# TensorE sums the squares of three norms between the last products of the layer before

## The chip, the cores and the metric

The kernel runs on one core of one Trainium2 chip. The time is the device time of one execution in microseconds (us). The engines are TensorE (PE, with its weight loads PEld), VectorE (DVE), ScalarE (ACT), GpSimd (POOL) and SyncE (SP), which issues most DMAs. Each engine works through its own instructions in order; semaphores tie them together.

## The reference

The reference is a two-layer diffusion backbone over 256 context and 256 latent tokens with 1024 features. Layer 0 has windowed attention beside a gated DeltaNet, layer 1 a Mamba-2 mixer, and each layer ends in a convolutional FFN. What matters here is the RMSNorm ahead of each projection and the residual that feeds it:

```python
def rms_norm(x, g):
    xf = x.astype(f32)
    y = xf * lax.rsqrt(jnp.mean(xf * xf, axis=-1, keepdims=True) + EPS)
    return (y * g.astype(f32)).astype(x.dtype)
...
        x = x + gt1 * m_lat
        x = x + gt2 * conv_ffn(modulate(rms_norm(x, norm_ffn_g[i]), sh2, sc2),
                               ffn_up[i], ffn_conv[i], ffn_down[i])
...
    return rms_norm(x, final_g)
```

The mean of the squares runs over all 1024 features of a token.

## The kernel before

The residual stream lies in SBUF as `xT`, features on the partitions, in eight blocks of 128 features by 512 tokens (256 context, 256 latent). A product that ends in the residual is a `RowGemm`. It reads the weights slot by slot. A slot holds two blocks of 128 input features, split into a high and a low part: ScalarE writes `w_hi`, VectorE writes `w_lo` (`split_lo`, line 304). TensorE makes three matmuls for each pair (high by high, L568; high by low activations, L571; low by high, L572). Except in the last slot it goes through the eight output blocks for each input block. In the last slot the output block m is outermost: six matmuls finish it and raise `mm_done`, then the next block follows. Each output block has one of the eight PSUM banks, in the order of `ROW_BANKS`: bank 4 for m = 0.

Behind each finished block comes a small pipeline. VectorE evicts the block into `xT` (L958; one instruction for each 256 tokens), ScalarE squares it into `norm_sq`, a ring of two buffers (L975), and VectorE adds the first six squared blocks into `norm_acc`, five additions in all (L982), each of them queued between two evictions. Ahead of the first eviction VectorE has one more weight split in its queue: that of the first slot of the next stage.

When all products are out, `Norm.pe_sums` has TensorE sum over the partitions with a matrix of ones: once for `norm_acc` (blocks 0 to 5), once for block 6 and once for block 7 (L1011). The output of each of the groups of 128 tokens goes to its own 32 partitions of bank 4, so a matmul there takes 32 columns of the array. An fp32 matmul stands as two records in the trace. ScalarE takes the root (L1018), VectorE the reciprocal (L1024), TensorE spreads the result over 128 partitions (`pe_spread`, L1030). Then VectorE and ScalarE make the modulated activations block by block (`norm_xn` L1044, `h_hi` L1063, `h_lo` L1052), TensorE multiplies the first weight slot with each block as it comes (`pe_first_slot`), and behind the last block VectorE splits the second weight slot, for which TensorE's next products wait.

Three norms are of this kind, each after a `RowGemm`: the first after the output projection of layer 0 (512 tokens, around 702 to 717 us of the profile), the second after the FFN of layer 0 (512 tokens, around 1075 to 1090), and the third after the output projection of layer 1 (256 tokens, around 1546 to 1555). The last norm (`Final`) uses the same class `Squares` but does its own sums. It is written as before in both kernels.

The order of each engine's work is written out by hand in `stage_layer0_tail` and `stage_layer1_tail`; there is no planner.

Of the kernel before, what the change touches and what calls it, by code (L numbers as in the profile page):

```python
# [19 lines left out]
P = 128  # L20
D = 1024
KD = D // P
# [101 lines left out]
class Tally:  # L124


    def __init__(self, sem):
        self.sem, self.base = sem, 0
# [7 lines left out]
    def take(self, n):  # L136

        self.base += n
        return Mark(self.sem, self.base - n)
# [116 lines left out]
def issue_loads(k, sp, upto):  # L256

    s = k.stream
    upto = min(upto, len(s.plan))
    while s.issued < upto:  # L260
        g = s.issued
        kind, n, parts = s.plan[g]
        if g >= 2:
            was, m, _ = s.plan[g - 2]
            if was == "split":
                sp.wait_ge(k.hi_done.sem, m + 1)
                sp.wait_ge(k.lo_done.sem, m + 1)
            else:
                sp.wait_ge(k.mod_used.sem, m + 1)
        for part in parts:  # L270
            if part[0] in ("rows", "rows4"):
                dst = s.raw[:, g % 2, :].rearrange("p (k n) -> p k n", k=4 if part[0] == "rows4" else 2)
                if part[1] is not None:
                    dst = dst[part[1] * HD:part[1] * HD + HD]
                src = part[2]
            else:
                (c0, w), src = part
                dst = s.raw[:, g % 2, :].rearrange("p (k n) -> p k n", k=KD)[:, :, c0:c0 + w]
            sp.dma_start(dst, src).then_inc(s.landed[g % 2], 16)
        s.issued += 1  # L280
# [683 lines left out]
class Squares:  # L964


    def __init__(self, k, row, sq, acc, sq_done, acc_done):
        self.k, self.row, self.sq, self.acc, self.sq_done, self.acc_done = k, row, sq, acc, sq_done, acc_done

    def act_square(self, act, m):  # L970
        k = self.k
        act.wait_ge(self.row.out_done.sem, self.row.out_done.at(m + 1))
        if m >= 2:
            act.wait_ge(self.acc_done.sem, self.acc_done.at(max(1, m - 2)))
        act.activation(self.sq[:, m % 2, :], k.xT[:, m, self.row.t0:T], ACT.Square).then_inc(self.sq_done.sem, 1)  # L975

    def dve_add(self, dve, j):
# [6 lines left out]
    def dve_evict_and_add(self, dve):  # L984
        for m in range(KD):
            self.row.dve_evict(dve, m)
            if 2 <= m <= 6:
                self.dve_add(dve, m - 1)


class Norm:
# [3 lines left out]
    def __init__(self, k, layer, which, row, hT, lT, b):  # L995
        self.k, self.layer, self.which, self.row = k, layer, which, row
        self.t0, self.n = row.t0, row.n
        self.hT, self.lT, self.xn, self.r = hT, lT, b.xn, b.r
        self.nt = self.n // P
        (sq_done, acc_done, self.sum_done, self.root_done, self.recip_done, self.spread_done, self.xn_done, self.hi_done,  # L1000
         self.lo_done) = take(k.tallies["norm"] + k.tallies["xnorm"], (KD, 5, 1, 1, 1, 1, KD, KD, KD))
        self.squares = Squares(k, row, b.sq, b.acc1, sq_done, acc_done)
        self.sum_bank, self.rstd_bank = k.pb[4], k.pb[5]

    def pe_sums(self, pe):
        k, q = self.k, self.squares
        parts = [(q.acc_done, 5, q.acc[:, :]), (q.sq_done, 7, q.sq[:, 0, :]), (q.sq_done, 8, q.sq[:, 1, :])]
        for i, (done, n, src) in enumerate(parts):
            pe.wait_ge(done.sem, done.at(n))
            for t in range(self.nt):  # L1010
                mm = pe.matmul(self.sum_bank[32 * t:32 * t + 32, 0:P], k.ones[:, 0:32], src[:, t * P:t * P + P],  # L1011
                               start=(i == 0), stop=(i == 2))
        mm.then_inc(self.sum_done.sem, 1)

    def act_root(self, act):
        k, rows = self.k, 32 * self.nt
        act.wait_ge(self.sum_done.sem, self.sum_done.at(1))
        act.activation(self.r[0:rows, :], self.sum_bank[0:rows, 0:P], ACT.Sqrt, bias=k.eps[0:rows, 0:1],  # L1018
                       scale=1.0 / D).then_inc(self.root_done.sem, 1)

# [301 lines left out]
class Final:  # L1322
# [18 lines left out]
    def pe_after(self, pe, m):  # L1341
        if m >= 5:
            self.pe_turn(pe, m - 5)
# [942 lines left out]
def stage_layer0_tail(k, a, g_out, g_up, g_down, g_ssm, cat, h, gh, gl, b):  # L2286


    nc = k.nc
    with ExitStack() as st:  # L2290
        row0 = RowGemm(k, 0, 2, g_out, 4, cat, 0, opens=True)
        norm1 = Norm(k, 0, 1, row0, h[0], h[1], b)
        up = FfnUp(k, 0, g_up, norm1, gh, gl, b.acc)
        down = RowGemm(k, 0, 5, g_down, KF // 2, lambda c: (gh(c), gl(c)), 0, up=up)
        norm2 = Norm(k, 1, 0, down, h[0], h[1], b)
        ssm = SsmIn(k, a, g_ssm, norm2, b)
        block = st.enter_context(nc.Block())

        @block.sync
        def _(sp):  # L2300
            issue_loads(k, sp, g_ssm + ssm.n_slots + 2)

        @block.tensor
        def _(pe):
            row0.pe(pe)
            norm1.pe(pe)
            up.pe(pe)
            down.pe(pe)
            norm2.pe(pe)
            ssm.pe(pe)  # L2310

        @block.scalar
        def _(act):
            row0.act_splits(act, 1, 5)
            norm1.act(act)
            up.act(act)
            down.act_splits(act, 1, KF // 2 + 1)
            norm2.act(act)
            ssm.act(act)

        @block.vector
        def _(dve):
            row0.dve_splits(dve, 1, 5)
            norm1.dve(dve)
            up.dve(dve)
            down.dve_splits(dve, 1, KF // 2 + 1)
            norm2.dve(dve)
            ssm.dve(dve)

    ssm.gates.end()  # L2330


def stage_layer1_tail(k, g_sout, g_up, g_down, y, h, gh, gl, b, out):

    nc = k.nc
    with ExitStack() as st:
        row1 = RowGemm(k, 1, 2, g_sout, SI // P // 2, y, LC, opens=True)
        norm = Norm(k, 1, 1, row1, h[0], h[1], b)
        up = FfnUp(k, 1, g_up, norm, gh, gl, b.acc)
        down = RowGemm(k, 1, 5, g_down, KF // 2, lambda c: (gh(c), gl(c)), LC, up=up)  # L2340
        fin = Final(k, down, b.sq, b.acc1, b.xs, b.xg, b.ss)
        block = st.enter_context(nc.Block())

        @block.sync
        def _(sp):
            issue_loads(k, sp, len(k.stream.plan))
            for h_ in range(2):
                sp.wait_ge(fin.y_done.sem, fin.y_done.at(h_ + 1))
                sp.dma_start(out[0, 0:P, h_ * 512:h_ * 512 + 512], fin.xg[:, 0, h_ * 512:h_ * 512 + 512]).then_inc(fin.s_out.sem, 16)
                sp.wait_ge(fin.y1_done.sem, fin.y1_done.at(h_ + 1))  # L2350
                sp.dma_start(out[0, P:2 * P, h_ * 512:h_ * 512 + 512], fin.xg[:, 1, h_ * 512:h_ * 512 + 512]).then_inc(fin.s_out.sem, 16)
            sp.wait_ge(fin.s_out.sem, fin.s_out.at(64))

        @block.tensor
        def _(pe):
            row1.pe(pe)
            norm.pe(pe)
            up.pe(pe)
            down.pe(pe, after=fin.pe_after)
            fin.pe_tail(pe)  # L2360

        @block.scalar
        def _(act):
            row1.act_splits(act, 1, SI // P // 2 + 1)
            norm.act(act)
            up.act(act)
            down.act_splits(act, 1, KF // 2)
            fin.act(act)

        @block.vector  # L2370
        def _(dve):
            row1.dve_splits(dve, 1, SI // P // 2 + 1)
            norm.dve(dve)
            up.dve(dve)
            down.dve_splits(dve, 1, KF // 2)
            fin.dve(dve)
# [196 lines left out]
```

## Time and profile before

| what | value |
|---|---|
| time, median of 3 runs | 1755.87 us (1751.68 to 1760.56) |
| profiled execution, time | 1765.24 us |
| its span, first to last instruction | 1763.2 us |
| mean granted TensorE clock, as a share of 2.4 GHz | 0.899 |
| TensorE busy (matmul) | 1525.8 us, 87% |
| VectorE busy | 989.7 us, 56% |
| ScalarE busy | 589.0 us, 33% |

The busy shares are those of the whole span. A norm takes some 15 us of it, so what limits a norm has to be read in its own stretch. The granted clock is either 1.00 or 0.50 at a given moment; a stretch with a change in it shows a value between.

### The profile page before, as it was taken

The page shows a single profiled execution, that of the slowest core. Times are in us where ns is not written, and L with a number is a line of the kernel's source. Part 1 is how long each engine was busy: PE and PEld are TensorE (multiplying, and loading weights), DVE is VectorE, ACT ScalarE, POOL GpSimd, SP SyncE. Part 2 cuts the span into 40 slices and gives each one's busy share as a digit, 9 for nine tenths or more (in the row PEclk, how much of TensorE's full clock was granted, in tenths as well). Part 3 has the DMA queues.
Part 4 walks back from the last instruction along what each step waited for, and adds up shares of the span by engine and source line. Part 5 has one row for each costly group of instructions (what it writes and reads, how often), then busy time and mean ns, then how long its engine had stood idle before and what let it go on. Part 6 is the DMA issues. An engine that isn't in the chain of part 4 may idle for free. (4 is left out here: it accounts for less than half of the span.)

```text
span 1763.2 us, 29502 instructions
## 1 busy us (share of the span) xinstructions
PE 1525.8 (87%) x12916; PEld 1252.5 (71%) x12916; DVE 989.7 (56%) x1457; ACT 589.0 (33%) x863; POOL 42.5 (2%) x42
## 2 busy tenths in 40 slices
PE   4499995779999759799999998999777975989998
PEld 2376772567777637688888886888755764979998
DVE  3346531464553452766555226767769666378854
ACT  2423435212222032533333113445211114355544
POOL 0000000000000000000000000000001210000000
PEclk8699997679999989899999998999897666989999
DMA  5622110025566203233332321322410000546653
GB/s 201 154 79 72 29 48 31 1 98 193 193 208 226 50 2 103 64 96 96 96 98 93 110 100 54 108 96 87 135 48 1 1 1 1 172 134 177 188 167 120
DMA packets 170618, 173.24 MB, mean 98 GB/s; under 512 B 15254, under 2 KB 135802, under 8 KB 170362
## 3 DMA queue, kind: packets, MB, share of 16 engines
q1 hardware_dynamic: 169184, 170.38, 31.0%
q8 instruction: 102, 1.67, 0.4%
q10 hardware_dynamic: 1306, 0.97, 0.2%
q14 instruction: 26, 0.21, 0.0%
HBM read 170.29 MB, written 1.05 MB: 97 GB/s over the span
## 5 line engine op out<-in xcount | busy, mean ns | idle before, releaser
L304 DVE TENSOR_TENSOR w_lo<-w_raw,w_hi 128x2048 fp32r<-128x2048 f32 x99 | 225.2, 2275 | 207.3 <-ACT w_hi L294 207.3
L568 PE MATMUL bank<-h_hi,w_hi 128*128 128x512 f32 (+1 forms) x904 | 316.1, 350 | 9.9 <-DVE h_lo L1052 7.5
L572 PE MATMUL bank<-h_hi,w_lo 128*128 128x512 f32 (+1 forms) x904 | 313.7, 347 | 0.0
L571 PE MATMUL bank<-h_lo,w_hi 128*128 128x512 f32 (+1 forms) x904 | 313.6, 347 | 0.0
L294 ACT ACTIVATE w_hi<-w_raw 128x2048 fp32r<-128x2048 f32 x99 | 187.9, 1898 | 225.0 <-PE bank L568 219.9
L586 DVE SCALAR_TENSOR_TENSOR acc<-bank,params,acc 128x510 f32<-128x510 f32 (+3 forms) x272 | 173.7, 646 | 131.1 <-ACT acc L1158 95.7
L568 PEld LDWEIGHTS bank<-h_hi,w_hi 128*128 128x128 f32 x904 | 173.1, 191 | 32.1 <-issue 11.7
L572 PEld LDWEIGHTS bank<-h_hi,w_lo 128*128 128x128 f32 x904 | 172.8, 191 | 21.2
L571 PEld LDWEIGHTS bank<-h_lo,w_hi 128*128 128x128 f32 x904 | 173.0, 191 | 20.5
L1158 ACT ACTIVATE acc<-bank,params 128x512 f32<-128x512 f32 (+1 forms) x88 | 49.3, 582 | 192.6 <-PE bank L572 90.8
L568 PE MATMUL bank<-h_hi,w_hi_hyb 128*128 128x512 f32 (+1 forms) x184 | 78.3, 426 | 21.9 <-PEq L476 19.8
L1653 PEld LDWEIGHTS bank<-inv_T,X_mat 64*64 64x64 f32 x1280 | 70.1, 136 | 13.2 <-issue 12.8
L1653 PE MATMUL bank<-inv_T,X_mat 64*64 64x64 f32 x1280 | 76.6, 225 | 1.2 <-issue 1.1
L571 PE MATMUL bank<-h_lo,w_hi_hyb 128*128 128x512 f32 (+1 forms) x184 | 74.5, 405 | 0.0
L572 PE MATMUL bank<-h_hi,w_lo_hyb 128*128 128x512 f32 (+1 forms) x184 | 74.3, 404 | 0.0
L1655 PE MATMUL bank<-X_mat,inv_T 64*64 64x64 f32 x1024 | 66.9, 223 | 2.0 <-issue 2.0
L1655 PEld LDWEIGHTS bank<-X_mat,inv_T 64*64 64x64 f32 x1024 | 62.7, 140 | 2.8 <-issue 2.8
L431 PE MATMUL bank<-w_raw,cond_padded 128*32 128x512 f32 x384 | 54.0, 673 | 9.4 <-DMA w_raw<-in_mod_w 7.2
L2124 PEld LDWEIGHTS bank<-x_dt,ssd_decay 128*128 128x128 f32 x256 | 41.0, 248 | 27.3 <-issue 21.6
L568 PEld LDWEIGHTS bank<-h_hi,w_hi_hyb 128*128 128x128 f32 (+1 forms) x184 | 35.6, 194 | 33.7 <-issue 23.1
L2124 PE MATMUL bank<-x_dt,ssd_decay 128*128 128x64 f32 x256 | 42.0, 334 | 19.9 <-DVE ssd_decay L2197 10.3
L304 DVE TENSOR_TENSOR w_lo_hyb<-w_raw,w_hi_hyb 128x2048 fp32r<-128x2048 f32 (+1 forms) x12 | 25.8, 2149 | 59.1 <-ACT w_hi_hyb L294 59.1
(349 smaller groups left out, 2881.9 us busy)
## 6 DMA issues: line engine op xcount, KB each, us to landing
w_raw<-in_mod_w SPq DMA_DIRECT2D x48, 1024.0 KB, 6.1
w_raw<-in_ffn_up SPq DMA_DIRECT2D x88, 512.0 KB, 5.1
w_raw<-in_ffn_down SPq DMA_DIRECT2D x22, 1024.0 KB, 4.9
w_raw<-in_ssm_w_in SPq DMA_DIRECT2D x20, 1024.0 KB, 5.2
w_raw<-in_hyb_w_in SPq DMA_DIRECT2D x9, 1024.0 KB, 5.1
w_raw<-in_ssm_w_out SPq DMA_DIRECT2D x8, 1024.0 KB, 4.9
w_raw<-in_hyb_w_in SPq DMA_DIRECT2D x8, 256.0 KB, 5.0
w_raw<-in_hyb_w_out SPq DMA_DIRECT2D x4, 512.0 KB, 7.9
```

Of the source, the lines that this page charges most:

```text
L294: act.activation(hi, raw, ACT.Copy).then_inc(k.hi_done.sem, 1)
L304: dve.tensor_tensor(lo, raw, hi.bitcast(F32), ALU.subtract).then_inc(k.lo_done.sem, 1)
L431: mm = pe.matmul(k.pb[7][32 * j:32 * j + 32, :], k.condpad[:, 4 * half + j, :], w[:, j, :], start=(half == 0), stop=(half == 1))
L568: mm = pe.matmul(out, wh, xh, start=(start and n == 0), stop=False)
L571: pe.matmul(out, wh, xl, start=False, stop=False)
L572: mm = pe.matmul(out, wl, xh, start=False, stop=(stop and n == last))
L586: ins = dve.scalar_tensor_tensor(out=ao, in0=bo, scalar=w(j), in1=ao, op0=ALU.mult, op1=ALU.add)
L1158: act.activation(acc[:, i % 4, :], self.bank(i), ACT.Copy, scale=self.taps(i)(1)).then_inc(self.seed_done.sem, 1)
L1653: mm = pe.matmul(YT(l)[q, r * DNC:r * DNC + DNC], Xm[q, l, r, :], d.TT[q, n, r, :], start=True, stop=True)
L1655: mm = pe.matmul(Y(l)[q, r * DNC:r * DNC + DNC], d.TT[q, n, r, :], Xm[q, l, r, :], start=True, stop=True)
L2124: mm = pe.matmul(k.pb[4 + q % 2][:, o:o + 64], dec[:, j % 2, dr, h, :], xdt[:, dr, (8 * g) * 64 + o:(8 * g) * 64 + o + 64], start=(dr == 0 ...
```

## The change

In the three norms TensorE now sums each of the eight squared blocks by itself: eight groups of matmuls of the ones matrix in place of three. The sums of blocks 0 to 5 stand in TensorE's queue inside the last slot of the products: behind the products of output block m comes the sum of squared block m - 2. Blocks 6 and 7 are summed after the last products. VectorE's five additions are gone, and `norm_acc` is no longer written by these norms. A buffer of `norm_sq` comes free when TensorE has summed it. The last norm keeps its additions.

```diff
@@ class Squares
-    def __init__(self, k, row, sq, acc, sq_done, acc_done):
+    def __init__(self, k, row, sq, acc, sq_done, acc_done, on_pe=False):
+        self.on_pe = on_pe
...
         act.wait_ge(self.row.out_done.sem, self.row.out_done.at(m + 1))
         if m >= 2:
-            act.wait_ge(self.acc_done.sem, self.acc_done.at(max(1, m - 2)))
+            act.wait_ge(self.acc_done.sem, self.acc_done.at(m - 1 if self.on_pe else max(1, m - 2)))
...
         for m in range(KD):
             self.row.dve_evict(dve, m)
-            if 2 <= m <= 6:
+            if 2 <= m <= 6 and not self.on_pe:
                 self.dve_add(dve, m - 1)
@@ class Norm
+    def pe_sum(self, pe, m):
+        k, q = self.k, self.squares
+        pe.wait_ge(q.sq_done.sem, q.sq_done.at(m + 1))
+        for t in range(self.nt):
+            mm = pe.matmul(self.sum_bank[32 * t:32 * t + 32, 0:P], k.ones[:, 0:32], q.sq[:, m % 2, t * P:t * P + P],
+                           start=(m == 0), stop=(m == KD - 1))
+        mm.then_inc(q.acc_done.sem, 1)
+
+    def pe_after(self, pe, m):
+        if m >= 2:
+            self.pe_sum(pe, m - 2)
+
     def pe_sums(self, pe):
-        k, q = self.k, self.squares
-        parts = [(q.acc_done, 5, q.acc[:, :]), (q.sq_done, 7, q.sq[:, 0, :]), (q.sq_done, 8, q.sq[:, 1, :])]
-        for i, (done, n, src) in enumerate(parts):
-            pe.wait_ge(done.sem, done.at(n))
-            for t in range(self.nt):
-                mm = pe.matmul(self.sum_bank[32 * t:32 * t + 32, 0:P], k.ones[:, 0:32], src[:, t * P:t * P + P],
-                               start=(i == 0), stop=(i == 2))
-        mm.then_inc(self.sum_done.sem, 1)
+        self.pe_sum(pe, 6)
+        self.pe_sum(pe, 7)
 
     def act_root(self, act):
...
-        act.wait_ge(self.sum_done.sem, self.sum_done.at(1))
+        act.wait_ge(self.squares.acc_done.sem, self.squares.acc_done.at(KD))
@@ stage_layer0_tail
-            row0.pe(pe)
+            row0.pe(pe, after=norm1.pe_after)
...
-            down.pe(pe)
+            down.pe(pe, after=norm2.pe_after)
@@ stage_layer1_tail
-            row1.pe(pe)
+            row1.pe(pe, after=norm.pe_after)
```

`RowGemm.pe` calls `after(pe, m)` behind the products of each output block of the last slot.

## Rows read from the trace of the kernel before

**Rows 1.** The page, part 1: busy time and share of each engine.

```profile
...
PE 1525.8 (87%) x12916; PEld 1252.5 (71%) x12916; DVE 989.7 (56%) x1457; ACT 589.0 (33%) x863; POOL 42.5 (2%) x42
...
```

**Rows 2.** Chain of work that ended last, behind the third norm: start, us, what.

```profile
...
1563.79 2.30 DVE w_lo L304
1566.23 0.36 PE bank L568
...
```

**Rows 3.** Timeline, first norm: start, us, engine, line, work [idle before <- releaser].

```profile
...
701.66 0.39 PE L572 MATMUL bank<-cat_dn_hi,w_lo 128*128 128x512 f32 x1
...
702.52 2.44 DVE L958 SCALAR_TENSOR_TENSOR xT<-bank,mod,xT 128x256 f32<-128x256 f32 x6
...
703.43 1.42 ACT L975 ACTIVATE norm_sq<-xT 128x512 f32<-128x512 f32 x2 [1.70 <-DVE xT L958]
...
708.46 0.39 PE L572 MATMUL bank<-cat_dn_hi,w_lo 128*128 128x512 f32 x1
...
711.09 0.87 DVE L958 SCALAR_TENSOR_TENSOR xT<-bank,mod,xT 128x256 f32<-128x256 f32 x2
...
711.23 0.43 PE L1011 MATMUL bank<-norm_acc,ones 128*32 128x128 f32 x8 [2.38 <-DVE norm_acc L982]
...
711.48 0.40 PE L1011 MATMUL bank<-norm_sq,ones 128*32 128x128 f32 x8
...
712.68 0.65 PE L1011 MATMUL bank<-norm_sq,ones 128*32 128x128 f32 x8 [0.80 <-ACT norm_sq L975]
...
714.81 2.08 PE L1030 MATMUL bank<-norm_r,base_consts 128*128 128x128 f32 x8 [1.48 <-DVE norm_r L1024]
...
```

**Rows 4.** Timeline, second norm, first squares.

```profile
...
1074.84 0.39 PE L572 MATMUL bank<-ffn_g_hi_b,w_lo 128*128 128x512 f32 x1
...
1076.60 0.63 ACT L975 ACTIVATE norm_sq<-xT 128x512 f32<-128x512 f32 x1 [1.70 <-DVE xT L958]
...
```

**Rows 5.** Timeline, second norm, VectorE's last eviction.

```profile
...
1084.26 0.48 DVE L958 SCALAR_TENSOR_TENSOR xT<-bank,mod,xT 128x256 f32<-128x256 f32 x1
...
```

**Rows 6.** Timeline of TensorE, third norm, end of the third product.

```profile
...
1543.73 0.28 PE L572 MATMUL bank<-y_hi,w_lo 128*128 128x256 f32 x1
...
```

**Rows 7.** Timeline of ScalarE, third norm, first squares.

```profile
...
1546.82 0.81 ACT L975 ACTIVATE norm_sq<-xT 128x256 f32<-128x256 f32 x2 [2.74 <-DVE xT L958]
...
```

**Rows 8.** Timeline, third norm, last eviction and spread.

```profile
...
1551.15 0.48 DVE L958 SCALAR_TENSOR_TENSOR xT<-bank,mod,xT 128x256 f32<-128x256 f32 x1
...
1554.21 1.22 PE L1030 MATMUL bank<-norm_r,base_consts 64*128 64x128 f32 x4 [1.44 <-DVE norm_r L1024]
...
```

**Rows 9.** Timeline of TensorE, modulation stage, between two tilings.

```profile
...
565.49 1.07 PE L431 MATMUL bank<-w_raw,cond_padded 128*32 128x512 f32 x8 [0.59 <-DMA w_raw<-in_mod_w]
566.49 0.34 PE L1653 MATMUL bank<-inv_T,X_mat 64*64 64x64 f32 x4
...
```

**Rows 10.** Timeline of TensorE, last FFN's products.

```profile
...
1692.77 0.28 PE L571 MATMUL bank<-ffn_g_lo,w_hi 128*128 128x256 f32 x1
1692.89 0.28 PE L572 MATMUL bank<-ffn_g_hi,w_lo 128*128 128x256 f32 x1
1695.14 0.36 PE L568 MATMUL bank<-ffn_g_hi,w_hi 128*128 128x256 f32 x1 [1.97 <-issue]
...
```

**Rows 11.** Busy time by stretch (the x is a count), PEclk is the granted clock.

```profile
...
core 0: us, PE busy (x) PEld busy (x) DVE busy (x) ACT busy (x) POOL busy (x), PEclk, DMA share, GB/s
...
1688.00:1695.40 7.40, 5.43 (x46) 5.26 (x45) 4.89 (x8) 2.94 (x4) 0.00 (x0) 1.00 0.34 135
1695.50:1698.80 3.30, 3.30 (x17) 3.30 (x17) 1.20 (x1) 1.91 (x1) 0.00 (x0) 0.50 0.80 238
1698.90:1705.00 6.10, 6.10 (x53) 6.10 (x53) 1.15 (x2) 1.92 (x1) 0.00 (x0) 1.00 0.62 208
...
```

**Rows 12.** The same view, two stretches after the first norm's products.

```profile
...
708.85:712.40 3.55, 0.65 (x17) 0.38 (x16) 3.11 (x7) 1.66 (x3) 0.00 (x0) 1.00 0.00 0
712.45:719.20 6.75, 2.73 (x16) 1.98 (x16) 3.04 (x7) 1.92 (x6) 0.00 (x0) 0.50 0.00 0
...
```

More of the change, by code:

```diff
@@ L1000, in __init__ @@
         (sq_done, acc_done, self.sum_done, self.root_done, self.recip_done, self.spread_done, self.xn_done, self.hi_done,
-         self.lo_done) = take(k.tallies["norm"] + k.tallies["xnorm"], (KD, 5, 1, 1, 1, 1, KD, KD, KD))
-        self.squares = Squares(k, row, b.sq, b.acc1, sq_done, acc_done)
+         self.lo_done) = take(k.tallies["norm"] + k.tallies["xnorm"], (KD, KD, 0, 1, 1, 1, KD, KD, KD))
+        self.squares = Squares(k, row, b.sq, b.acc1, sq_done, acc_done, on_pe=True)
         self.sum_bank, self.rstd_bank = k.pb[4], k.pb[5]
-    def pe_sums(self, pe):
-        k, q = self.k, self.squares
-        parts = [(q.acc_done, 5, q.acc[:, :]), (q.sq_done, 7, q.sq[:, 0, :]), (q.sq_done, 8, q.sq[:, 1, :])]
-        for i, (done, n, src) in enumerate(parts):
-            pe.wait_ge(done.sem, done.at(n))
-            for t in range(self.nt):
-                mm = pe.matmul(self.sum_bank[32 * t:32 * t + 32, 0:P], k.ones[:, 0:32], src[:, t * P:t * P + P],
-                               start=(i == 0), stop=(i == 2))
-        mm.then_inc(self.sum_done.sem, 1)
+    def pe_sum(self, pe, m):
[8 more added lines that the diff above has]
+            self.pe_sum(pe, m - 2)
+    def pe_sums(self, pe):
+        self.pe_sum(pe, 6)
+        self.pe_sum(pe, 7)
     def act_root(self, act):
         k, rows = self.k, 32 * self.nt
-        act.wait_ge(self.sum_done.sem, self.sum_done.at(1))
+        act.wait_ge(self.squares.acc_done.sem, self.squares.acc_done.at(KD))
         act.activation(self.r[0:rows, :], self.sum_bank[0:rows, 0:P], ACT.Sqrt, bias=k.eps[0:rows, 0:1],
```

## The prediction

> **What bounds the kernel now.** The page's busy shares come first: TensorE is busy for 87% of the span [rows 1], so almost everywhere a delay of TensorE is a delay of the end. The chain of waits comes second. Behind the third norm it runs through VectorE's split of the second weight slot (1563.79, 2.30 us) into TensorE's next products at 1566.23 [rows 2]. That split stands behind the eight modulated blocks in VectorE's queue, and they stand behind the spread of the root. So whatever moves the spread moves the next stage by the same amount, and the first slot's products, which run beside the modulation, do not set its end. The timeline comes third, for what sets the spread. In the first norm TensorE has issued its last product matmul at 708.46 (it ends 0.39 later, at 708.85), while VectorE starts its last eviction only at 711.09 [rows 3]. VectorE is behind: its first eviction starts at 702.52, because a weight split stands ahead of it, and three evictions take 2.44 us, 0.81 each. Seven steps of 0.81 would be 5.7 us; the last eviction starts 8.57 us after the first, and the difference, 2.9 us, is the five additions (0.58 each). From the last eviction the path is eviction, square, sum, root, reciprocal, spread.
>
> So the change takes work off the engine that is late. The question is what it puts on TensorE, and where.
>
> **What TensorE waits for.** The sum of block 0 stands behind the third product block. In the first norm that block's last matmul starts at 701.66 and ends at 702.05. The square of block 0 starts at 703.43 [rows 3] and one of 512 tokens takes 0.63 [rows 4]. From the end of the last eviction (711.96) to the last sum (712.68) pass 0.72 us: a square and two handovers, 0.05 each [rows 3]. So the first sum can start at 703.43 + 0.63 + 0.05 = 704.11, and TensorE, which before worked through, stands 2.06 us with products 3 to 7 queued behind. The removed additions do not help here: the first of them came after three evictions. In the second norm it is the same: block 2 ends at 1074.84 + 0.39 = 1075.23, the sum can start at 1076.60 + 0.63 + 0.05 = 1077.28 [rows 4], a stall of 2.05. In the third (256 tokens) block 2 ends at 1544.01 [rows 6], the square starts at 1546.82 and takes half of 0.81 [rows 7], so the sum starts at 1547.28, a stall of 3.27. Who is late next: product blocks 3 to 7, and with them VectorE's last five evictions.
>
> **What a sum costs between products.** Two groups of sums in a row start 0.25 us apart at the full clock (711.23, 711.48) [rows 3]; four matmuls of 32 columns each run at the same time, so the third norm with two of them pays the same. Turning from 32-column tiles to another tiling costs more: eight records of 512 columns start at 565.49 and the next tiling at 566.49 [rows 9]. By the sums' price those columns are four times 0.22 plus a start of 0.03, 0.91; the turn is the remaining 0.09, rounded to 0.10. I take that for the turn back too. The first product after a break takes 0.36 in place of 0.28 [rows 10]: 0.08 more for a weight load that nothing hides. A sum between products is 0.25 + 0.10 + 0.10 + 0.08 = 0.53 us; the first one, after a stall, has no turn into it: 0.43. From below the turns are free and a sum is 0.25. From above each turn waits out a whole matmul (0.39), and a sum is 1.11. I take 0.53, since the row that shows a turn is nearest to it.
> The Trainium skill, TensorEngine Tiling (Array Packing), Key Properties, says that a change of the tiling mode drains the engine. It speaks against this change: without a drain the sums cost 3.7 us in all below, with it 7.6. The trace agrees with a drain, at 0.09 us for the turn that it shows.
>
> **The sum, norm by norm, at the full clock.** From matmul 18 of the last slot (701.66) to matmul 48 (708.46) are 6.80 us, which is the work of product blocks 3 to 7 [rows 3]. Their last matmul ends 0.39 - 0.23 = 0.16 after its slot in the stream. With four more sums between the five blocks the last product is done at 704.11 + 0.43 + 6.80 + 4 x 0.53 + 0.16 = 713.62, and the last eviction starts 0.05 later, at 713.67, against 711.09: **2.58 us later**. The evictions of 0.87 and squares of 0.63 keep up with a product block every 1.89, so TensorE alone paces it. The sum of block 5 is done before the last square is. Second norm: 1077.28 + 9.51 + 0.05 = 1086.84 against 1084.26 [rows 5]: 2.58. Third: the matmuls start 0.12 apart [rows 10], 30 of them are 3.60; 1547.28 + 0.43 + 3.60 + 2.12 + 0.16 + 0.05 = 1553.64 against 1551.15 [rows 8]: 2.49. Together +7.6 us (7.65).
>
> **The clock.** Two terms more. First, a stall inside the products can bring the granted clock down from 2.4 to 1.2 GHz. In the last FFN TensorE stood from 1693.17 to 1695.14, 1.97 us [rows 10]. The clock was 1.00 before, 0.50 in 1695.5 to 1698.8, and 1.00 after, and TensorE got 17 matmuls done in those 3.3 us where at the rate after (53 in 6.1) it would be 29 [rows 11]: 12 x 0.12 = 1.4 us lost, or half of 3.3, 1.65. I take 1.6 for each fall. The stalls here are 2.05, 2.06 and 3.27 us. I take the longest and one of the other two: +3.2. Bounds: none, 0; three, +4.8. Second, today the clock falls at the end of the norm: 1.00 until 712.4 with TensorE 0.65 us busy in 3.55, then 0.50 [rows 12]. The last sum takes 0.65 where at the full clock one takes 0.40 (0.25), and the spread takes 2.08 [rows 3], in the third norm 1.22 [rows 8], half of it at the full clock. After the change TensorE has just finished its products when the last square comes (some 1.5 us later), so the last sum most likely runs at the full clock in all three: -0.75. For the spread it is open, as TensorE idles again during root and reciprocal; I take it as won in one large and in the third norm: -1.04 - 0.61. Together -2.4. Bounds: 0 and -3.4.
>
> **Nothing else moves.** No DMA is added or moved; the weights' release comes with the first matmul of the slot, ahead of the stall, so SyncE's queue is untouched. ScalarE's squares wait for a sum in place of an addition and are not late by it. VectorE's added idle time is worth nothing.
>
> Sum: 7.6 + 3.2 - 2.4 = **+8.4 us** on the profiled execution's 1765.24. It lies 9.4 us above the median of the runs, and most of that has nothing to do with three norms, so I put the 8.4 on the median: 1755.87 + 8.4 = **1764.3 us**.
>
> **Rivals.**
> - *Turns are free* (a sum is 0.25): 0.18 + 4 x 0.28 = 1.30 less per norm, 3.9 in all: +4.5, 1760.4 us. Against it speaks the turn seen, though in another pair of tilings.
> - *The clock holds through the stalls*: 7.6 - 2.4 = +5.2, 1761.1 us. For it: two stalls are barely longer than 2 us. Against it: the fall after 1.97 us.
> - *The clock falls in all three and nothing is won at the end*: 7.6 + 4.8 = +12.4, 1768.3 us. It takes no more than the same row three times.
> - *The first sum never waits* (faster). If the squares were ready when block 2 ends, only five sums of 0.53 would push the products: the last eviction at 708.85 + 2.65 + 0.05 = 711.55 (+0.46), in the second norm 6.80 + 2.70 after 1075.23, 1084.73 (+0.47), in the third the products, before done 30 x 0.12 after 1544.01 at 1547.61, at 1550.31 (-0.84). That is +0.1, and with the whole clock gain -3.3: 1752.6 us. With free turns as well (about -7.4) it would near the faster side of what can be told. It needs the first eviction 2.06 us earlier, in the third norm 3.27; the sign turns at a stall of about 1.1 us per norm (3.3 / 3). The split ahead of the evictions is not moved, so I give it little.
>
> **How the numbers follow.** A measurement of this kernel tells no change from about 0.5%, 8.8 us. Forecast (one or two falls of the clock, +6 to +11) 0.50; free turns 0.16; clock holds 0.12; three falls 0.18; first sum without a wait 0.04. The forecast's interval lies about half above 8.8: slower 0.22 + 0.18 = 0.40, rounded up to 0.42 for turns dearer than 0.10. The last rival alone reaches beyond 8.8 on the faster side only with free turns, so faster is 0.03 at most; same 0.55. The range goes from the free turns with the clock gain taken at its best (3.7 - 3.4, about 0) and a little of the runs' own scatter to the three falls and as much: 1757 to 1770 us. Turns of 0.39, some +15, are left out.
>
> **What would show it.** TensorE's timeline in the last slot: a gap of about 2.05, 2.05 and 3.3 us behind matmul 18, named as a wait for ScalarE's square; five groups of sums at some 0.5 us each between product blocks; the last eviction (L958) waiting for a matmul and no longer for its own queue; the granted clock at 0.50 somewhere behind a gap; spreads nearer 1 than 2 us. From the last split's end to the spread's start some 2.5 us more in each norm. The prediction fails if the gaps are missing, if a sum between products is far from 0.5, or if the delay is swallowed ahead of the second slot's products.

## The result

The changed kernel takes 1765.45 us in the median (1763.98 to 1772.70, 8 runs), the kernel before 1755.09 (1749.29 to 1760.56, 8 runs). The ratio is 1.0065, with a 95% interval of 1.0042 to 1.0088: slower by 11.4 us, between 7.4 and 15.5. The two medians differ by 10.4 us; every such difference in us in this document is the ratio's, taken on the median of the kernel before. The forecast was +8.4 us and 1764.3 us.

The first view is the page of the kernel after: its head and the busy time of the engines.

```profile
span 1764.3 us, 29675 instructions
...
PE 1531.7 (87%) x13016; PEld 1251.2 (71%) x13016; DVE 982.7 (56%) x1442; ACT 588.4 (33%) x863; POOL 42.5 (2%) x42
...
```

The span is only about 1 us longer than that of [rows 1]'s execution, and TensorE's share is the same. The two spans can't be held against each other for this change: before's profiled execution was a long one of its kind (1765.24 us against a median of 1755), and the first norm's last slot begins at 692.23 here and at 697.81 there, ahead of anything that was changed. So each norm is measured by itself, from the first product matmul of the last slot to the first matmul of the second weight slot of the next stage:

| us from first matmul of the last slot to | norm 1 before | norm 1 after | norm 2 before | norm 2 after | norm 3 before | norm 3 after |
|---|---|---|---|---|---|---|
| last eviction | 13.28 | 17.60 | 13.28 | 16.16 | 9.45 | 13.38 |
| spread | 17.00 | 21.09 | 17.00 | 19.65 | 12.52 | 16.21 |
| second slot's first matmul | 35.79 | 39.89 | 35.80 | 38.44 | 24.53 | 28.23 |

The last line adds up to 96.12 us before and 106.56 after. The three norms alone are 10.4 us longer, and that is the measured slowdown within its interval.

Next the second norm in TensorE's timeline of the kernel after. It is the one in which the clock stayed up. L1010 are the sums, L1037 is the spread.

```profile
...
1073.37 0.39 PE L572 MATMUL bank<-ffn_g_hi_b,w_lo 128*128 128x512 f32 x1
1075.81 0.43 PE L1010 MATMUL bank<-norm_sq,ones 128*32 128x128 f32 x8 [2.06 <-ACT norm_sq L976]
...
1077.43 0.39 PE L572 MATMUL bank<-ffn_g_hi_b,w_lo 128*128 128x512 f32 x1
1077.75 0.43 PE L1010 MATMUL bank<-norm_sq,ones 128*32 128x128 f32 x8
...
1085.24 0.39 PE L572 MATMUL bank<-ffn_g_hi_b,w_lo 128*128 128x512 f32 x1
1085.56 0.65 PE L1010 MATMUL bank<-norm_sq,ones 128*32 128x128 f32 x16
1087.26 0.42 PE L1010 MATMUL bank<-norm_sq,ones 128*32 128x128 f32 x8 [1.05 <-ACT norm_sq L976]
1089.16 2.07 PE L1037 MATMUL bank<-norm_r,base_consts 128*128 128x128 f32 x8 [1.48 <-DVE norm_r L1031]
```

Product block 2 ends at 1073.37 + 0.39 = 1073.76, and then TensorE does nothing until 1075.81, when the first square is there (before, products ran through here, [rows 4]). From there a sum stands between product blocks with a period of 1.94 us (1075.81, 1077.75) in place of 1.36. The spread takes 2.07 us, as in [rows 3].

VectorE in the same stretch:

```profile
...
1072.02 2.29 DVE L304 TENSOR_TENSOR w_lo<-w_raw,w_hi 128x2048 fp32r<-128x2048 f32 x1 [8.59 <-ACT w_hi L294]
1074.23 2.44 DVE L958 SCALAR_TENSOR_TENSOR xT<-bank,mod,xT 128x256 f32<-128x256 f32 x6
1077.86 0.88 DVE L958 SCALAR_TENSOR_TENSOR xT<-bank,mod,xT 128x256 f32<-128x256 f32 x2 [1.20 <-PE bank L572]
...
1085.67 0.88 DVE L958 SCALAR_TENSOR_TENSOR xT<-bank,mod,xT 128x256 f32<-128x256 f32 x2 [1.08 <-PE bank L572]
...
```

Ahead of the first eviction stands the weight split (1072.02, 2.29 us). Three evictions run in a row as before, then each waits about 1.1 us for TensorE's matmul (L572). Before, the last one waited for VectorE's own queue [rows 3, 5]. The engine that was late is now idle, and the engine that has the products is late.

The busy time by stretch, with the granted clock (the number behind the ACT count and POOL's), for the first, second and third norm:

```profile
...
696.40:698.50 2.10, 0.07 (x1) 0.00 (x0) 2.10 (x5) 0.63 (x1) 0.00 (x0) 1.00 0.05 14
699.65:703.00 3.35, 3.35 (x15) 1.95 (x14) 0.88 (x2) 1.02 (x2) 0.00 (x0) 0.50 0.77 216
703.05:709.70 6.65, 6.65 (x46) 4.01 (x45) 2.63 (x6) 1.90 (x3) 0.00 (x0) 1.00 0.01 2
...
1073.80:1075.80 2.00, 0.00 (x0) 0.00 (x0) 2.00 (x6) 0.63 (x1) 0.00 (x0) 1.00 0.23 30
1075.85:1085.60 9.75, 9.75 (x74) 6.03 (x76) 4.32 (x11) 3.79 (x6) 0.00 (x0) 1.00 0.31 103
1085.65:1088.70 3.05, 0.98 (x24) 0.44 (x24) 1.42 (x3) 1.00 (x2) 0.00 (x0) 1.00 0.00 0
1088.80:1090.00 1.20, 0.84 (x4) 0.84 (x5) 0.31 (x1) 0.00 (x0) 0.00 (x0) 0.50 0.00 0
...
1542.55:1545.80 3.25, 0.00 (x0) 0.00 (x0) 3.17 (x4) 0.51 (x3) 0.00 (x0) 1.00 0.47 124
1546.15:1549.50 3.35, 3.35 (x17) 2.74 (x16) 0.48 (x1) 0.84 (x3) 0.00 (x0) 0.50 0.99 282
...
```

The gaps are there in all three. In the first norm the clock was 0.50 from 699.65 to 703.00, with TensorE at work (15 matmul records in 3.35 us, eight of them those of a sum); in the second it stayed at 1.00; in the third it was 0.50 from 1546.15 to 1549.50. At the end of the norm it fell again, in the second between 1088.70 and 1088.80, just ahead of the spread. The first norm's spread, at 713.32, was slow as well (TensorE's timeline):

```profile
...
713.32 2.08 PE L1037 MATMUL bank<-norm_r,base_consts 128*128 128x128 f32 x8 [1.47 <-DVE norm_r L1031]
...
```

The sums of the third norm, in TensorE's timeline of the kernel after. From 1546.15 to 1549.50 the clock is 0.50, behind that it is 1.00:

```profile
...
1545.82 0.41 PE L1010 MATMUL bank<-norm_sq,ones 128*32 128x128 f32 x4 [3.27 <-ACT norm_sq L976]
...
1547.74 0.64 PE L1010 MATMUL bank<-norm_sq,ones 128*32 128x128 f32 x4
...
1549.76 0.41 PE L1010 MATMUL bank<-norm_sq,ones 128*32 128x128 f32 x4
...
1550.99 0.41 PE L1010 MATMUL bank<-norm_sq,ones 128*32 128x128 f32 x4
...
1552.24 0.41 PE L1010 MATMUL bank<-norm_sq,ones 128*32 128x128 f32 x4
...
1554.59 0.41 PE L1010 MATMUL bank<-norm_sq,ones 128*32 128x128 f32 x4 [0.46 <-ACT norm_sq L976]
...
```

At the full clock a product block of 256 tokens and its sum take 1.25 us (1550.99, 1552.24), where six product matmuls 0.12 apart are 0.72: a sum costs 0.53 here.

### The profile page after: what moved, and what is told of

Read it like the earlier page. It is cut to its first block and busy times, and to the rows that moved or that the text cites. A ratio compares the mean times of both kernels' runs of the same rounds, so it can differ in the third digit from the quotient of the medians.

```text
span 1764.3 us, 29675 instructions
## 1 busy us (share of the span) xinstructions
PE 1531.7 (87%) x13016; PEld 1251.2 (71%) x13016; DVE 982.7 (56%) x1442; ACT 588.4 (33%) x863; POOL 42.5 (2%) x42
## 3 DMA queue, kind: packets, MB, share of 16 engines
HBM read 170.29 MB, written 1.05 MB: 97 GB/s over the span
## 5 line engine op out<-in xcount | busy, mean ns | idle before, releaser
L572 PE MATMUL bank<-h_hi,w_lo 128*128 128x512 f32 (+1 forms) x904 | 313.6, 347 | 0.0
L572 PEld LDWEIGHTS bank<-h_hi,w_lo 128*128 128x128 f32 x904 | 172.8, 191 | 21.6
L572 PE MATMUL bank<-h_hi,w_lo_hyb 128*128 128x512 f32 (+1 forms) x184 | 73.2, 398 | 0.0
```

Source lines behind the costliest of these rows:

```text
L572: mm = pe.matmul(out, wl, xh, start=False, stop=(stop and n == last))
```

## The experiments

Six more kernels ran, each beside the kernel before on the same chip. The column "norms" is the sum over the three norms of the stretch above, from one profiled execution, less the 96.12 us of the kernel before.

| kernel | ratio to before (95%) | us from it | norms, us |
|---|---|---|---|
| changed kernel | 1.0065 (1.0042 to 1.0088) | +11.4 | +10.4 |
| e1: all sums behind the products | 0.9935 (0.9914 to 0.9956) | -11.4 | -9.5 |
| e2: e1 and the wait alone | 1.0008 (0.9986 to 1.0030) | +1.4 | +0.9 |
| e3: e1 and sums five blocks behind | 0.9967 (0.9946 to 0.9988) | -5.8 | -6.3 |
| e5: changed kernel, weight split behind the evictions | 1.0022 (0.9999 to 1.0046) | +3.9 | +2.9 |
| e6: changed kernel, idle filled at the end | 1.0071 (1.0037 to 1.0106) | +12.5 | +9.6 |
| e4: e1, idle filled at the end | 0.9947 (0.9930 to 0.9964) | -9.3 | -9.4 |

**e1: all sums behind the products.** The squares get eight buffers, so neither ScalarE nor TensorE has to wait for the other until the end:

```diff
-            act.wait_ge(self.acc_done.sem, self.acc_done.at(m - 1 if self.on_pe else max(1, m - 2)))
-        act.activation(self.sq[:, m % 2, :], ...
+            if not self.on_pe:
+                act.wait_ge(self.acc_done.sem, self.acc_done.at(max(1, m - 2)))
+        act.activation(self.sq[:, m % (8 if self.on_pe else 2), :], ...
...
     def pe_after(self, pe, m):
-        if m >= 2:
-            self.pe_sum(pe, m - 2)
+        pass
 
     def pe_sums(self, pe):
-        self.pe_sum(pe, 6)
-        self.pe_sum(pe, 7)
+        for m in range(KD):
+            self.pe_sum(pe, m)
```

> All eight sums of a norm stand behind the last product, none between products; the squares have a buffer each, so that no square waits. Theory (the time went into TensorE's wait inside the products, the turns of tiling between them, and the clock's falls behind the wait): no gap inside the products; the last eviction starts with the last product's end, about 2.15 us earlier than in the kernel before in each norm, and the last sum runs at the full clock (0.25 us less): about -7 us against the kernel before, 1748. Rival (the additions' removal or something outside the norms made it slower, not the place of the sums): about +10 us against the kernel before, as in the changed kernel.

Measured: 1745.63 us in the median, 0.9935. TensorE's timeline of the second norm in e1:

```profile
...
1065.91 0.39 PE L572 MATMUL bank<-ffn_g_hi_b,w_lo 128*128 128x512 f32 x1
1066.23 2.13 PE L1011 MATMUL bank<-norm_sq,ones 128*32 128x128 f32 x64
1069.84 1.16 PE L1037 MATMUL bank<-norm_r,base_consts 128*128 128x128 f32 x8 [1.48 <-DVE norm_r L1031]
```

VectorE's, and the busy time by stretch behind the products:

```profile
...
1066.34 0.88 DVE L958 SCALAR_TENSOR_TENSOR xT<-bank,mod,xT 128x256 f32<-128x256 f32 x2 [0.48 <-PE bank L572]
...
```

```profile
...
1066.30:1069.80 3.50, 2.06 (x65) 1.56 (x64) 1.83 (x3) 1.22 (x3) 0.00 (x0) 1.00 0.02 5
1069.80:1071.00 1.20, 1.16 (x8) 0.97 (x8) 0.00 (x0) 0.00 (x0) 0.00 (x0) 1.00 0.00 0
...
```

The last eviction starts with the end of the last product (1066.34 against 1065.91 + 0.39); in the third norm, where the products are shorter, VectorE is still 1.4 us behind. All eight sums take 2.13 us, 64 records, most of it in time in which TensorE had nothing else. The spread takes 1.16 us with the clock at 1.00, and so in all three norms (1.16, 1.16, 0.71). The rival falls: the additions' removal is worth 2.2 us a norm once nothing takes their place on TensorE. The gain is larger than I expected (-11.4 against -7, the norms -9.5) by the spreads at the full clock (0.92 + 0.92 + 0.51 = 2.4 us), which I had left open.

**e2: the wait alone.** As e1, and behind the third product block TensorE waits for the first square without summing it:

```diff
     def pe_after(self, pe, m):
-        pass
+        if m == 2:
+            pe.wait_ge(self.squares.sq_done.sem, self.squares.sq_done.at(1))
```

> As e1, but TensorE waits for the first square behind the third product block, without any sum there. Theory: gaps of 2.06, 2.06 and 3.27 us stand behind matmul 18 of the last slot; the last eviction starts 2.06 us (3.27 less 1.4 of cover by VectorE's evictions in the third norm) later than in e1, plus up to 1.7 us for each fall of the clock: +6 to +11 us against e1, so about +2 us against the kernel before. Rival (the sums' own time and turns cost it, the wait is covered by VectorE's lateness): the same time as e1 within 1 us.

Measured: 1.0008, +1.4 us, that is +12.8 against e1 by the ratios (11.5 by the medians) and +10.4 by the norms. Busy time by stretch in e2, first, second and third norm:

```profile
...
697.85:699.80 1.95, 0.00 (x0) 0.00 (x0) 1.95 (x5) 0.61 (x1) 0.00 (x0) 1.00 0.07 20
701.05:704.35 3.30, 3.30 (x10) 2.53 (x9) 0.88 (x2) 0.97 (x2) 0.00 (x0) 0.50 0.78 221
...
1071.70:1073.60 1.90, 0.00 (x0) 0.00 (x0) 1.90 (x5) 0.59 (x1) 0.00 (x0) 1.00 0.22 13
1073.70:1080.70 7.00, 7.00 (x30) 5.55 (x30) 4.35 (x11) 3.48 (x6) 0.00 (x0) 1.00 0.43 145
1540.70:1543.90 3.20, 0.00 (x0) 0.00 (x0) 3.14 (x4) 0.46 (x3) 0.00 (x0) 1.00 0.59 164
1544.10:1547.40 3.30, 3.30 (x16) 3.30 (x17) 1.09 (x3) 1.06 (x4) 0.00 (x0) 0.50 0.94 271
...
```

The gaps are back, with no matmul in them, and behind them the clock fell in the first and the third norm, not in the second. The second norm gives the price of the wait at the full clock: 34.81 - 32.45 = 2.36 us for a gap of 2.06. The first gives 36.43 - 32.45 = 3.98, so the fall cost 1.62. The rival, that VectorE's lateness covers the wait, falls. The +1.4 against the kernel before is not told apart from zero: the wait alone eats what taking the additions away gives.

**e3: sums between products, without a wait.** As e1, and the sums of blocks 0 to 2 stand behind product blocks 5 to 7:

```diff
     def pe_after(self, pe, m):
-        pass
+        if m >= 5:
+            self.pe_sum(pe, m - 5)
 
     def pe_sums(self, pe):
-        for m in range(KD):
+        for m in range(3, KD):
             self.pe_sum(pe, m)
```

> As e1, but the sums of blocks 0 to 2 stand behind the products of blocks 5 to 7: turns between products without a wait in the norms of 512 tokens (the third norm keeps some 1.3 us of it). Theory: each sum between products costs 0.58 us (a period of 1.95 us per product block and sum, against 1.36 for the block alone); the last eviction starts 1.2 us later than in e1: about +3 us against e1, -4 against the kernel before. Rival (a sum between products costs only its columns, 0.22 us): +1 us against e1.

Measured: 0.9967, -5.8 us; against e1 the norms are 3.2 us longer. TensorE's timeline of the second norm in e3:

```profile
...
1068.06 0.39 PE L572 MATMUL bank<-ffn_g_hi_b,w_lo 128*128 128x512 f32 x1
1068.37 0.43 PE L1011 MATMUL bank<-norm_sq,ones 128*32 128x128 f32 x8
1068.73 0.50 PE L568 MATMUL bank<-ffn_g_hi_b,w_hi 128*128 128x512 f32 x1
1069.07 0.39 PE L571 MATMUL bank<-ffn_g_lo_b,w_hi 128*128 128x512 f32 x1
...
1070.32 0.43 PE L1011 MATMUL bank<-norm_sq,ones 128*32 128x128 f32 x8
...
```

From the last product of a block to the sum are 0.31 us where 0.23 is the pace (a turn of 0.08), the sum's columns take until the next product at 1068.73, 0.36 later, and from that product to the next 0.34 in place of 0.23. From one sum to the next are 1.95 us, 0.59 more than six products. The last product comes 1.19 us later than in e1 (11.84 against 10.65 from the slot's first), with two sums ahead of it. So a sum in the stream costs 0.59 us, not its 0.22 of columns, and the rival falls. In the third norm a wait of 1.11 us is left ahead of the first of the three sums; its last eviction comes 0.85 later than in e1.

**e5: the changed kernel without its wait.** VectorE's weight split for the next stage moves from ahead of the first eviction to behind the last, in all three norms:

```diff
-            row0.dve_splits(dve, 1, 5)
-            norm1.dve(dve)
+            row0.dve_splits(dve, 1, 4)
+            norm1.dve(dve, lambda: row0.dve_splits(dve, 4, 5))
...
-    def dve(self, dve):
+    def dve(self, dve, split):
         self.squares.dve_evict_and_add(dve)
+        split()
         self.dve_recip(dve)
```

> The changed kernel with one thing moved: VectorE's weight split that stood ahead of the first eviction now stands behind the last. Theory: the first square is ready when the third product block ends, so there is no gap and no fall of the clock inside the products, but all six sums stand between them: last eviction 0.7 us later than in the kernel before, and the split behind it costs up to 0.7 us more ahead of the reciprocal: about +2.5 us against the kernel before, some 8 us less than the changed kernel. Rival (the sums and their turns are the cost): no better than the changed kernel, about +10 us.

Measured: 1.0022, +3.9 us (between -0.2 and +8.1), the norms +2.9. TensorE's timeline of the second norm in e5, and VectorE's:

```profile
...
1069.71 0.42 PE L1010 MATMUL bank<-norm_sq,ones 128*32 128x128 f32 x8 [0.25 <-ACT norm_sq L976]
...
1071.65 0.43 PE L1010 MATMUL bank<-norm_sq,ones 128*32 128x128 f32 x8
...
```

```profile
...
1079.56 0.88 DVE L958 SCALAR_TENSOR_TENSOR xT<-bank,mod,xT 128x256 f32<-128x256 f32 x2 [1.08 <-PE bank L572]
1080.36 2.28 DVE L304 TENSOR_TENSOR w_lo<-w_raw,w_hi 128x2048 fp32r<-128x2048 f32 x1
1082.56 0.94 DVE L1031 RECIPROCAL norm_r<-norm_r 128x128 f32<-128x128 f32 x1
```

The gap of 2.06 us is 0.25 now, and the clock did not fall inside the products of any of the three norms. That takes 7.6 us off the changed kernel's norms. All sums still stand between the products (1.94 us from one to the next), so the last eviction starts 14.35 us after the slot's start, 1.07 later than in the kernel before, where 0.7 was expected; in the third norm it starts 0.35 earlier. The split behind it holds the reciprocal back by 0.5 (3.99 us from last eviction to spread, against 3.49 in the changed kernel), in the third norm by 0.77 (3.60 against 2.83). Without the split's share, 1.8 of the 2.9, the norms would still be 1.1 us longer than before. Sums between products with next to no wait are still no gain.

**e6: the idle time at the end filled.** The changed kernel, with matmuls whose output nobody reads:

```diff
         self.pe_sum(pe, 6)
+        if self.n == T:
+            self.fill(pe, 3)
         self.pe_sum(pe, 7)
+        self.fill(pe, 5 if self.n == T else 6)
+
+    def fill(self, pe, count):
+        for i in range(count):
+            pe.matmul(self.k.pb[6][:, 0:self.n], self.k.whi[:, 0, 0:P], self.k.whi[:, 0, 0:self.n], start=True, stop=True)
```

> The changed kernel with matmuls that serve nothing in TensorE's idle time at the end of each norm: three between the sums of blocks 6 and 7 in the two norms of 512 tokens, and five (six in the third norm) between the last sum and the spread. Theory (the spread ran at 1.2 GHz because TensorE stood idle from its products to the spread, in two pieces): the spread takes 1.16 us in place of 2.08 in the two norms and 0.71 in place of 1.22 in the third, so about -2.3 us against the changed kernel, and the gap and the fall inside the products stay. Rival (the fall inside the products or the sums between them bring the clock down whatever stands behind): the spread stays at 2.08 and the time is that of the changed kernel or up to 1 us more for the fillers.

Measured: 1.0071, with an interval that holds the changed kernel's ratio; the times do not tell the two apart, and the 2.3 us that were expected do not show in them. The trace does tell the mechanism. TensorE's timeline at the end of the second norm (L1027 are the fillers, L1044 the spread), and a stretch behind that norm's gap:

```profile
...
1083.32 0.96 PE L1027 MATMUL bank<-w_hi 128*128 128x512 f32 x3
1084.44 0.43 PE L1010 MATMUL bank<-norm_sq,ones 128*32 128x128 f32 x8 [0.17 <-ACT norm_sq L976]
1084.80 1.45 PE L1027 MATMUL bank<-w_hi 128*128 128x512 f32 x5
1086.34 1.16 PE L1044 MATMUL bank<-norm_r,base_consts 128*128 128x128 f32 x8
```

```profile
...
1071.70:1075.00 3.30, 3.30 (x18) 1.88 (x14) 0.70 (x2) 1.21 (x2) 0.00 (x0) 0.50 0.90 302
...
```

The spread takes 1.16 us, in the first norm too, and 0.71 in the third, as the theory had it; the rival on the spread falls. From last eviction to the second slot's first matmul the norms are about 2.3 us shorter for it. But in this execution the clock fell behind all three gaps, the second norm's too (0.50 from 1071.7 to 1075.0), and that gave 1.44 of the 2.3 back.

**e4: fillers where the clock is up already.** e1 with six such matmuls between the last sum and the spread:

```diff
     def pe(self, pe):
         self.pe_sums(pe)
+        for i in range(6):
+            pe.matmul(self.k.pb[6][:, 0:512], self.k.whi[:, 0, 0:P], self.k.whi[:, 0, 0:512], start=True, stop=True)
         self.pe_spread(pe)
```

> e1 with six matmuls that serve nothing between the last sum and the spread. Theory: in e1 the spread already ran at the full clock in all three norms, so the fillers win nothing: the time of e1 within 1 us, or up to 0.3 us per norm more for the turns. Rival (e1 was lucky with the clock in its profiled execution and mostly pays 2.08 us for the spread): up to 2.3 us less than e1.

Measured: 0.9947, the norms 86.67 us against e1's 86.60. As expected, nothing is won. In e1 TensorE's idle time from the sums to the spread was one piece of 1.48 us, and the clock lived through it without help.

## Why the prediction was right, and where it was off

**The wait behind product block 2** was the right step. Predicted gaps 2.06, 2.05 and 3.27 us; measured 2.06, 2.06 and 3.27. e2 shows what it costs alone and e5 what the changed kernel is without it.

**The cost of a sum between products** was predicted at 0.53 us for all three norms. It is 0.58 to 0.59 in the norms of 512 tokens and 0.53 in the third. The turns were priced about right from the one turn that the trace showed; what was missed is that the product matmuls of 512 columns behind a sum start 0.233 us apart, not 0.227, and that the first of them is 0.34 in front of the second, 0.11 over the pace and not 0.08. The Trainium skill's page TensorEngine Tiling (Array Packing) states under Key Properties that a change of the tiling mode drains the engine. The 0.08 to 0.11 us that each turn adds here agree with it; no run shows that a drain is what takes them. So the last evictions came 2.88 us later at the full clock in the norms of 512 tokens (norm 1: 4.32 less its fall of 1.44), where 2.58 was predicted, and 2.49 us later in the third (3.93 less its fall of 1.44), as predicted.

**The falls of the clock** came as the forecast's case had it: behind the longest gap and one of the other two. They cost 1.44 us in the first norm (the two norms of 512 tokens differ by that and by nothing else) and as much in the third (two product blocks with their sums took 1.92 and 2.02 us in place of 1.25 each); in e2's first norm, 1.62. Predicted 1.6. Over the profiled executions of the changed kernel, e2 and e6, one of each, the clock fell behind 4 of 6 gaps of 2.06 us and behind 3 of 3 gaps of 3.27 us. Which one it is varies from execution to execution: e6 has the changed kernel's gaps, and its execution had three falls. That the profiled execution of the changed kernel had just two, the case that the sum took, is therefore partly luck.

**The gain at the end was the step that failed in size**: -2.4 predicted, -0.7 measured. The last sum did run at the full clock in all three norms: from last eviction to spread 0.22, 0.23 and 0.24 us less, predicted 0.25. The spread was to be won in two of three and was won in none. In the changed kernel TensorE idles 1.05 us before the last sum and 1.48 behind it (0.46 and 1.44 in the third norm), and the clock fell 0.05 to 0.4 us before the spread began. e6 shows that it is this idle time: filled (in the third norm only behind the last sum), the three spreads take 1.16, 1.16 and 0.71 us. The price of a won spread was a little too high as well: half of 2.08 and of 1.22 was taken, and the full clock gives 0.92 and 0.51.

The sum by measured terms is: evictions 4.32 + 2.88 + 3.93 = 11.13, of which 2.9 for the two falls, less 0.69 at the end: 10.4, against 7.6 + 3.2 - 2.4 = 8.4. The missing 2.0 us are the spreads (1.65) and the evictions (11.13 against 10.8). The forecast time of 1764.3 us lies only 1.2 us under the measured 1765.45, closer than the change itself, because it was added to a median of the kernel before (1755.87) that was 0.8 us over the one of this comparison.

**The rivals.** Free turns are ruled out by e3. That the clock holds through the stalls is ruled out for the three profiled executions that have them, though in two of them one gap passed. Three falls did occur, in e6. The first sum without a wait is e5, +3.9 us with the split's own cost of 0.5 us in the norms of 512 tokens and 0.77 in the third; it never came near faster. Its last evictions moved by +1.07, +1.07 and -0.35 us, where this rival had +0.46, +0.47 and -0.84, and its spreads were not won either (2.07, 2.07 and 1.22).

That the slowdown sits in the three norms is shown by the norms' stretches, which agree with the times within their intervals for all seven kernels; these intervals are some 6 to 12 us wide, so an effect of a microsecond or two elsewhere could hide in them. Where the clock falls in the runs that have no profile was not seen. The two longest runs of the changed kernel (1772.70 and 1771.50 us) also have the lowest mean granted clock (0.894 and 0.897, against 0.900 to 0.903 in the other six), so there was more time at half clock in them. Whether it was a third fall in a norm is open.

## What to carry to other kernels

Work moved to the engine that bounds the kernel has to go where that engine is idle, not where it is merely ahead: with six of the eight sums between the last products the norms are 10.4 us longer, and with all eight behind the products they are 9.5 us shorter. With the wait nearly gone (e5) the sums between the products still gain nothing. The first thing to look up for a consumer that is put into an in-order queue is the time at which its producer is ready, worked out from the producer's own queue: the producer here stood behind an unrelated weight split of 2.29 us. And more buffers (eight squares for two) are what lets the sums move behind the products: by the code, with two buffers the third square would wait for the first sum. No run tried it so.

## What the runs showed that was not expected

The granted clock made a difference of 0.92 us in each spread of eight records (2.08 against 1.16 us) and 0.51 in one of four (1.22 against 0.71), and whether it was up went with what TensorE had done just before: up after one idle piece of 1.48 us directly behind 2.13 us of sums (e1), down after 1.05 us idle, a sum of 0.42 and 1.48 us idle (changed kernel). Two idle pieces alone do not decide it. In e3's second norm the clock stayed up through 0.40 and 1.48 us, with 40 records of sums ahead of them, while in the changed kernel's third norm it fell after 0.46 and 1.44 us:

```profile
...
1072.28 1.30 PE L1011 MATMUL bank<-norm_sq,ones 128*32 128x128 f32 x40
1073.98 0.43 PE L1011 MATMUL bank<-norm_sq,ones 128*32 128x128 f32 x8 [0.40 <-ACT norm_sq L977]
1075.88 1.16 PE L1038 MATMUL bank<-norm_r,base_consts 128*128 128x128 f32 x8 [1.48 <-DVE norm_r L1032]
...
```

What makes the difference between these two no run separates. A gap of 2.06 us inside a dense stream was followed by a stretch at half clock (the rows of 3.30 and 3.35 us above) in 4 cases of 6, so a short wait in TensorE's stream, priced alone in e2, cost 2.36 us where the clock held and 3.98 where it fell, never 2.06.
